# Choice of tokens in a mixture of experts: 175 products of a mask put between TensorE's needed ones

## What is computed

```python
def expert_choice_ffn(h, w_router, w_gate, w_up, w_down):
    B, N, D = h.shape
    cap = EC_CAPACITY_FACTOR * N // N_EXPERTS            # 256
    aff = jax.nn.softmax((h @ w_router).astype(jnp.float32), axis=-1)
    g, idx = lax.top_k(jnp.swapaxes(aff, 1, 2), cap)     # 256 tokens for each of 16 experts
    xs = jax.vmap(lambda hb, ib: hb[ib])(h, idx)
    hid = jax.nn.silu(jnp.einsum('becd,edf->becf', xs, w_gate)) * jnp.einsum('becd,edf->becf', xs, w_up)
    ys = jnp.einsum('becf,efd->becd', hid, w_down) * g[..., None].astype(h.dtype)
    return jax.vmap(lambda yb, ib: jnp.zeros((N, D), yb.dtype).at[ib.reshape(-1)].add(yb.reshape(-1, D)))(ys, idx)
```

## Time and profile before

| what | value |
|---|---|
| median of 3 runs | 3531.86 us |
| the profiled execution | 3532.93 us, its span 3531.1 us |
| mean granted clock of TensorE | 0.976 of full |
| PE busy | 3348.5 us, 95% |
| DVE (VectorE) busy | 1931.3 us, 55% |
| ACT (ScalarE) busy | 1378.3 us, 39% |
| the choice, first to last product (L2518 to L2576) | 2322.39 to 2372.58 us |

### The profile page before, as it was taken

One profiled execution on the slowest core, in us unless ns is written; L12 is line 12 of the kernel. 1 busy time (PEld: TensorE's weight loads), 2 busy tenths in 40 slices (PEclk: granted clock), 3 DMA queues, 4 the chain that ended last, 5 costly groups with the idle time before them and its releaser, 6 DMA issues. The chain is left out here.

```text
span 3531.1 us, 75240 instructions
## 1 busy us (share of the span) xinstructions
PE 3348.5 (95%) x31534; PEld 2871.7 (81%) x31534; DVE 1931.3 (55%) x3276; ACT 1378.3 (39%) x1973; POOL 559.9 (16%) x792
## 2 busy tenths in 40 slices
PE   7999999999799998989999989959999999999997
PEld 5778888787677877878888878849999999999997
DVE  4666766667445655762212236666656665666563
ACT  5445454444255655330000013424444444444442
POOL 3555545564100000000000000000000100010000
PEclk9999999999899999999999999959999999999999
DMA  4221222211233434331111135426666666666662
GB/s 144 56 83 50 71 68 68 77 50 44 65 126 125 138 126 138 133 94 30 50 39 30 49 107 173 160 95 226 203 217 211 203 203 215 213 202 205 212 214 72
DMA packets 361219, 439.96 MB, mean 125 GB/s; under 512 B 15236, under 2 KB 300196, under 8 KB 360100
## 3 DMA queue, kind: packets, MB, share of 16 engines
q1 hardware_dynamic: 351784, 403.20, 35.3%
q0 software_dynamic: 9216, 33.56, 4.1%
HBM read 369.59 MB, written 67.13 MB: 124 GB/s over the span
## 5 line engine op out<-in xcount | busy, mean ns | idle before, releaser
L2655 PE MATMUL bank<-ex_x_hi,ex_w_lo 128*128 128x256 f32 x2048 | 581.4, 284 | 2.0 <-DVE ex_x_lo L2837 2.0
L2656 PE MATMUL bank<-ex_x_lo,ex_w_hi 128*128 128x256 f32 x2048 | 580.2, 283 | 0.0
L2657 PE MATMUL bank<-ex_x_hi,ex_w_hi 128*128 128x256 f32 x2048 | 580.1, 283 | 0.0
L2651 DVE TENSOR_TENSOR ex_w_lo<-ex_w_loaded,ex_w_hi 128x2048 fp32r<-128x2048 f32 x192 | 434.0, 2289 | 226.9 <-ACT ex_w_hi L2647 222.5
L2647 ACT ACTIVATE ex_w_hi<-ex_w_loaded 128x2048 fp32r<-128x2048 f32 x192 | 359.4, 1905 | 173.3 <-PE bank L2657 169.3
L2655 PEld LDWEIGHTS bank<-ex_x_hi,ex_w_lo 128*128 128x128 f32 x2048 | 393.6, 192 | 2.8 <-issue 2.2
L2656 PEld LDWEIGHTS bank<-ex_x_lo,ex_w_hi 128*128 128x128 f32 x2048 | 393.7, 192 | 0.6
L2657 PEld LDWEIGHTS bank<-ex_x_hi,ex_w_hi 128*128 128x128 f32 x2048 | 393.7, 192 | 0.0
L2711 POOL CAST ex_idx<-moe_idx_all 128x2 uint32 (+1 forms) x16 | 3.0, 186 | 1777.6 <-POOLq L79 1466.3
L264 PE MATMUL bank<-columns_columns_hi,weights_weights_lo 128*128 128x512 f32 x544 | 226.9, 417 | 8.9 <-DVE columns_columns_lo L848 3.8
L2811 ACT ACTIVATE ex_hid_hi<-ex_hidden 128x256 fp32r<-128x256 f32 x128 | 53.4, 417 | 414.0 <-DVE ex_hidden L2860 414.0
(11 more groups left out here) (474 smaller groups left out, 8265.4 us busy)
## 6 DMA issues: line engine op xcount, KB each, us to landing
ex_w_loaded<-in_wg SPq DMA_DIRECT2D x64, 1024.0 KB, 5.3
ex_w_loaded<-in_wu SPq DMA_DIRECT2D x64, 1024.0 KB, 6.8
ex_w_loaded<-in_wd SPq DMA_DIRECT2D x64, 1024.0 KB, 5.0
plain_weights<-in_w_in SPq DMA_DIRECT2D x70, 512.0 KB, 4.7
gl_ada_tile<-in_ada_w SPq DMA_DIRECT2D x48, 512.0 KB, 4.3
plain_columns<-hT_dram SPq DMA_DIRECT2D x14, 1024.0 KB, 7.4
sc_w_loaded<-in_sc_w_in SPq DMA_DIRECT2D x23, 512.0 KB, 6.5
plain_columns<-in_x SPq DMA_DIRECT2D x16, 512.0 KB, 5.5
```

The source lines that it names most:

```text
L2651: nc.vector.tensor_tensor(w_lo[c % SPLIT][:], raw[:, c % LOADED, :], w_hi[c % SPLIT][:].bitcast(F32), ALU.subtract).then_inc(s["lo"], 1)
L2655: nc.tensor.matmul(psum, ll, rh, start=first, stop=False)
L2656: nc.tensor.matmul(psum, lh, rl, start=False, stop=False)
L2657: return nc.tensor.matmul(psum, lh, rh, start=False, stop=last)
```

## The change

A helper `keep_awake(products)` multiplies the rounded mask by itself, 128 x 128 by 128 columns, into the first 128 columns of bank 7, as often as it is told. It is called with 40 ahead of the first round and with 9 behind L2528 of each of the 15 rounds. Nothing reads bank 7 there, and no semaphore is waited for or raised by these products.

```diff
                 mm.then_inc(s["spread"], 1)
                 pe.wait_ge(s["consts"], 16)
                 pe.wait_ge(s["rounded"], 6)
+                def keep_awake(products):
+                    for _ in range(products):
+                        nc.tensor.matmul(bank[7][:, 0:P], same_r[:], same_r[:], start=True, stop=True)
+                keep_awake(40)
                 for r in range(HIGH + LOW):
                     at = sums[r % 2]
                     nc.tensor.matmul(at, same_r[:], base[:], start=True, stop=False)
@@
                     nc.tensor.matmul(at, less_r[:], signs[:], start=False, stop=False)
                     pe.wait_ge(s["counted"], r + 1)
                     nc.tensor.matmul(at, same_r[:], cnt[:], start=False, stop=True).then_inc(s["summed"], 1)
+                    keep_awake(9)
                 pe.wait_ge(s["listed"], 1)
```

## The result

The changed kernel takes 3544.24 us (median of 7 runs, 3543.05 to 3545.77) against 3533.32 for the kernel before, run beside it (7 runs, 3530.76 to 3537.07). The ratio is 1.0031, with a 95% interval of 1.0021 to 1.0041: **slower by 10.9 us**. The forecast was no difference; the first rival, at 3543.2 us, is what happened. The spans of the profiled executions are 3541.8 and 3531.1 us, 10.7 apart.

The account below looks back on a forecast made before the run. The choice's rounds were taken as bound by a chain across engines, with PE at half clock only 0.50 of 1.84 us; +0.8 - 1.0 - 0.1 = -0.3 us gave 3531.5 us, own range 3529 to 3534, with rivals to 3545.

Parts of the forecast that it names:

- the first rival: In the choice of tokens: added products leave the clock at half and delay needed ones, +11.3, 3543.2 us; chance 0.26.
- The chain of a round: Search rounds: 1.84 us each, PE's part only 0.50 us; VectorE waited for it 3.0 us in all.
- The price of a product: Each added 128-column fp32r product on PE: 0.213 us at half clock, 0.111 at full.
- the dearer price of plain f32: Added products cost 0.43 us at half clock, 0.24 at full, though the clock rises: +13.5, 3545.4 us; chance 0.10.
- The forty: Batch ahead of round 0: clock rises after 5.2 us, batch ends 7.0 us after its start.
- The term of +0.8 us: Round 0: VectorE's first read of the sum comes at 2333.0 instead of 2332.16, behind the forty.
- The nines: Each round: 12 products' weights take 1.33 us at full clock, so nine end about 0.4 us before the next signs.
- What a full clock gives back: Needed products in the rounds: 0.10 us in each of the 10 rounds that wait, -1.0 us.
- The rival: Same as the first rival: clock stays low, L2528 +3.4 late, 13 intervals 33.3 us, together +11.3; chance 0.26.
- A clock once full was to be lost between 2362 and 2369: Behind the last round: PE has little to do until L2535 at 2367.13, so only -0.1 us counted there.
- the wide one: Range of the whole kernel's time including the rivals: 3529 to 3545 us.
- The two cases behind "slower by over 0.2%": Whole kernel: clock stays low (3543.2 us, chance 0.26) or dearer product (3545.4 us, 0.10); given together as 0.35.

Follow-up runs that it names:

- e7_short_22_2: The change with 22 added products ahead of the search and 2 a round instead of 40 and 9; 3532.73 us, ratio 0.9996 to the kernel before.
- e3: The change with added products of 512 columns instead of 128, 10 ahead and 4 a round; 3534.17 us, ratio 0.9997 to the kernel before.
- e5: The change with added products of 256 columns instead of 128, still 40 and 9; 3534.69 us, ratio 1.0000 to the kernel before.
- e10: The kernel before plus 256-column products in the choice's idle times, more 512-column ones during the gather and seven before the first expert; 3531.70 us, ratio 0.9993.
- e8_bf16_40_9: The change with the mask of the added products in bf16, still 40 and 9 of 128 columns; 3536.06 us, one run.
- e1_forty_only: The change with only the 40 products ahead of the search, none in the rounds; 3533.95 us, ratio 1.0002 to the kernel before.
- e2: The change with only the nine products in each round, none ahead of the search; 3541.26 us, ratio 1.0018 to the kernel before.
- e4: The change with dense rounded affinities instead of the mask as both operands of the added products; 3543.23 us, one run.
- e6: The change with added products of 256 columns, 20 ahead instead of 40, still 9 a round; 3534.33 us, ratio 1.0004 to the kernel before.

## Why the prediction was wrong, step by step

- **The chain of a round** was read right. PE is not what a round waits for while products fit (e7_short_22_2), and the gain from a full clock is 0.10 us a round, 1.84 to 1.74 (e3, e5, e10).
- **The price of a product**, 0.213 us at half clock from the rows of 2 and of 256 columns, was right to the last digit, and the dearer price of plain f32 is out. The 0.111 at full clock came from transposes and stays untried, since no fp32r product of 128 columns ever ran at a full clock. The Trainium skill (TensorE: Matmul & The Clock Gate, What you observe) has its 107 ns from products in bf16. The runs agree with it for bf16, 0.107 us in e8_bf16_40_9. The Trainium skill's section LDWEIGHTS, on the same page, reckons a load by its columns alone, which is 107 ns for 128. Here a four-byte product takes twice that, 0.213 us with 4, with 128 and with 256 columns alike; that it is the load which takes this time is inferred from that and not measured by itself.
- **The forty** is the step that failed: "How soon does the clock rise under a steady train?" I took 4.4 and 6.1 us from trains of 512 columns and set the time of a train of 128 columns equal to them. It never rose. The clock stood at 0.50 for all 8.76 us of the forty and for the rounds behind them. The term of +0.8 us measured +2.7 (VectorE's first read, e1_forty_only). The prediction's own doubt, "that these are fp32r, with a weight load as long as the product or longer, keeps it open", was the right question, and got 0.26. What I set against it, 64 short instructions from 888.2 to 891.4 ahead of a rise, was no train of this shape: they stand 3.2 / 64 = 0.05 us apart.
- **The nines**, "1.33 us, less than 1.84", rested on the full clock and fell with it: 2.56 us a round, +7.9.
- **What a full clock gives back**, -1.0, was not there, as the clock it needs wasn't. In e5, where the clock was full, the late rounds had it (1.74 us), and those of the second search at half clock took more than it back: its choice is 51.20 us.
- **The rival**, that the clock stays low, had each part: L2532 3.4 us late (measured 3.4), 13 intervals of 33.3 us (33.3), together +11.3 (+11.3 in the choice, +10.9 in the median).
- A clock once full was to be lost between 2362 and 2369, and e5 lost it at 2366.2. That nothing here can win more than 4 us has held in all runs.
- The time lies outside the forecast's own range of 3529 to 3534 us; the wide one reaches it only for the rivals' sake. The two cases behind "slower by over 0.2%" add up to 0.36, not 0.35.

## What to carry to other kernels

Work that is only there to keep a clock up stands in the same queue as work that is waited for: price it at the low clock, where it will first run, and let it fit there. To judge whether it will raise the clock, look for a train of the same shape and type in the trace, not only for a busy engine. Compare what the clock can give per round with what a late product costs: here 0.10 us against 0.72.

## What the runs showed of the hardware

- TensorE was busy 47 of 49 us, nearly all of it with products of 128 x 128 by 128 columns in fp32r, and its granted clock stayed at 0.50 (the change; e2 and e4 alike); dense numbers instead of a mask made no difference.
- With 256 columns instead of 128 a product took the same 0.213 us at half clock, and the clock rose 2.9 us after the first. At half clock the second 128 columns of an fp32r product were free (e5).
- In bf16, products of 128 columns were 0.107 us apart at half clock, and the clock rose 3 us after the first (e8).
- Nine products of 256 columns a round went with a full clock in intervals of 1.74 to 2.03 us (e5), where PE never idled over 0.28 us. It was lost in e6 after 1.40 us of idle time ahead of round 0's sum and in e10 after 0.82 us in round 1. But later in e10 it stayed full over idle times of 0.35 and 0.85 us, and before the first expert it fell in some kernels and not in others after the same 1.97 us. The length of one idle time doesn't decide it by itself, and what does wasn't tried apart.
